# FFN products by one level of Strassen's method, with the activations' sums kept in DRAM

## The chip, the cores and the metric

The kernel runs on one core of a Trainium2 chip. The metric is the device time of one execution in microseconds (us). The engines are named as the profile names them: PE is TensorE, DVE is VectorE, ACT is ScalarE, POOL is GpSimd, SP is SyncE; PEld is PE's weight load, which overlaps its matmuls.

## What is computed

One layer: attention and a state-space mixer in parallel, then the FFN that the change is about, on 1280 tokens (1024 latent, 256 context), D_MODEL 1024 and D_FF 2816.

```python
def ffn_sublayer(x, shift, scale, gate, g_pre, g_post, w_gate, w_up, w_down):
    h = rms_norm(x, g_pre) * (1 + scale) + shift
    f = (jax.nn.silu(h @ w_gate) * (h @ w_up)) @ w_down
    return x + gate * rms_norm(f, g_post)
```

All of it is float32. The kernel gets that precision from float32r operands in two parts: each value is split into a rounded `hi` and a rest `lo`, and a product is three matmuls, hi by hi, lo by hi and hi by lo, summed in PSUM (`split3`, L404 to L408). ACT makes the hi part by a copy, DVE the lo part by a subtraction.

## The kernel before

The phases run one after another, each with one instruction stream an engine, ordered by semaphores. A phase ends when all its engines have ended.

**Output projection** (`phase_out_proj`, L1650). Ten token tiles of 128. For each, PE does 48 matmuls of 512 columns into `psY`. ACT squares and sums (L1743), DVE scales and adds the residual into `y` (L1777, L1781), SP stores `y`, ACT squares again (L1748), and DVE writes the normalised tile to `facc` (L1786). POOL makes the two powers in between (L1719, L1721).

**FFN** (`phase_ffn`, L1805). First the normalised tiles are transposed and modulated: `Turn` has 24 steps (three token blocks of 512, 512 and 256 by eight K tiles); a step is two to four transposes on PE (L148), one ACT (L159) and two DVE instructions (L167, L169). Eight steps stand before the first product, the rest are woven into the first F tiles. Then a loop runs over eleven pairs of F tiles (`over_pairs`). Each F tile of 128 multiplies all tokens: for each block, gate and up, eight K tiles by three matmuls into `psG`; ACT takes the silu (L1886), DVE multiplies (L1920), and both split the result (L1888, L1923). After a pair come 20 down products of six matmuls with 512 columns into `psF`, which DVE adds to `facc` (L1938). SP loads the weights of the pair to come as soon as DVE has taken the lo part of the last.

**Final** (`phase_final`, L1995). The down products of the last pair, ten tiles of 12 matmuls; DVE adds them to `facc` (L2054), ACT squares, POOL makes the power (L2036), DVE scales (L2068), and DVE and POOL in turn add the residual that SP has loaded from `y1` (L2012). SP stores the rows.

## Time and profile before

| | |
|---|---|
| median of 3 runs | 1998.24 us (1996.91 to 2000.24) |
| span of the profiled execution | 1999.9 us |
| PE busy | 1822.0 us (91%), 9587 instructions |
| DVE busy | 900.2 us (45%) |
| ACT busy | 538.4 us (27%) |
| POOL busy | 111.5 us (6%) |
| DMA | 130.97 MB, mean 65 GB/s |
| mean granted TensorE clock | 0.964 |

The span runs from the first to the last instruction of one profiled execution; it lies 1.7 us over the median and within the three runs. Busy times are shares of the span. A matmul's row is longer than the time until the next one begins, since matmuls overlap in the array: the pace of PE is read from the starts, or from something that recurs once a tile. The granted clock is a share of 2.4 GHz; its two levels are 1.00 and 0.50. A releaser (`<-`) is what an engine's idle time ended on.

### The profile page before, as it was taken

The numbers are of one execution on the slowest core, as the hardware profiler recorded it, in microseconds if no ns is written. First come the engines' busy times: TensorE is split into PE (matmuls) and PEld (weight loads), VectorE is DVE, ScalarE is ACT, GpSimd is POOL, SyncE is SP. The second block draws the span as 40 slices with busy tenths as digits, with TensorE's granted clock in tenths as the row PEclk, the third lists the DMA queues.
The fourth block names the chain that finished last, engine by engine and source line by source line (L and its number), as shares of the span: only waits on it lengthen the run. The fifth ranks groups of instructions, "written<-read, shape, count | busy, mean of one in ns | idle before, by whom it ended". The sixth has DMA issues, their size and how long they took to land. (4 is left out here: it accounts for less than half of the span.)

```text
span 1999.9 us, 23563 instructions
## 1 busy us (share of the span) xinstructions
PE 1822.0 (91%) x9587; PEld 1549.0 (77%) x9596; DVE 900.2 (45%) x1240; ACT 538.4 (27%) x770; POOL 111.5 (6%) x130
## 2 busy tenths in 40 slices
PE   5899999778858989986988999999999999999995
PEld 5688888656647777875867888888888888888884
DVE  6635753267754454445445414334143242332418
ACT  5442222132334343443324111111111112011112
POOL 1000000213300000000100000000000000000005
PEclk8899999878979999998999999999999999999997
DMA  8423322110040000005321010010100100001006
GB/s 282 157 86 128 135 95 80 48 47 18 28 147 17 1 12 1 1 1 189 120 102 64 32 64 32 31 56 19 51 31 31 63 31 31 31 31 63 11 25 227
DMA packets 66854, 130.97 MB, mean 65 GB/s; under 512 B 7232, under 2 KB 40592, under 8 KB 66784
## 3 DMA queue, kind: packets, MB, share of 16 engines
q1 hardware_dynamic: 62176, 122.52, 17.8%
q0 software_dynamic: 4608, 7.47, 1.1%
q8 instruction: 50, 0.82, 0.2%
q14 instruction: 20, 0.16, 0.0%
HBM read 108.87 MB, written 21.09 MB: 65 GB/s over the span
## 5 line engine op out<-in xcount | busy, mean ns | idle before, releaser
L406 PE MATMUL psG<-h_hi,gu_hi 128*128 128x512 f32 (+1 forms) x1056 | 373.9, 354 | 0.0
L407 PE MATMUL psG<-h_lo,gu_hi 128*128 128x512 f32 (+1 forms) x1056 | 373.6, 354 | 0.0
L408 PE MATMUL psG<-h_hi,gu_lo 128*128 128x512 f32 (+1 forms) x1056 | 373.5, 354 | 0.0
L406 PEld LDWEIGHTS psG<-h_hi,gu_hi 128*128 128x128 f32 x1056 | 199.7, 189 | 27.9
L407 PEld LDWEIGHTS psG<-h_lo,gu_hi 128*128 128x128 f32 x1056 | 199.7, 189 | 27.8
L408 PEld LDWEIGHTS psG<-h_hi,gu_lo 128*128 128x128 f32 x1056 | 199.6, 189 | 27.5
L1920 DVE TENSOR_TENSOR hid<-hid,psG 128x512 f32<-128x512 f32 (+1 forms) x66 | 39.5, 599 | 359.2 <-ACT hid L1886 359.2
L1938 DVE TENSOR_TENSOR facc<-facc,psF 128x512 f32<-128x512 f32 x180 | 122.9, 687 | 94.3 <-PE psF L408 94.3
L406 PE MATMUL psP<-hT_hi,win_hi 128*128 128x512 f32 (+1 forms) x456 | 163.0, 357 | 0.8 <-DVEq L678 0.8
L407 PE MATMUL psP<-hT_lo,win_hi 128*128 128x512 f32 (+1 forms) x456 | 161.7, 355 | 0.0
L408 PE MATMUL psP<-hT_hi,win_lo 128*128 128x512 f32 (+1 forms) x456 | 161.7, 354 | 0.0
L406 PE MATMUL psF<-d_hi,h_hi 128*128 128x512 f32 x400 | 155.7, 389 | 0.0
L407 PE MATMUL psF<-d_lo,h_hi 128*128 128x512 f32 x400 | 155.7, 389 | 0.0
L408 PE MATMUL psF<-d_hi,h_lo 128*128 128x512 f32 x400 | 155.6, 389 | 0.0
L1886 ACT ACTIVATE hid<-psG 128x512 f32<-128x512 f32 (+1 forms) x66 | 34.8, 527 | 392.3 <-PE psG L408 392.3
L1878 ACT ACTIVATE d_hi<-raw_d 128x1024 fp32r<-128x1024 f32 x22 | 23.3, 1060 | 290.8 <-PE psF L408 241.4
L406 PEld LDWEIGHTS psP<-hT_hi,win_hi 128*128 128x128 f32 x456 | 86.5, 190 | 13.7 <-DVEq L678 1.2
L407 PEld LDWEIGHTS psP<-hT_lo,win_hi 128*128 128x128 f32 x456 | 86.5, 190 | 12.0
L408 PEld LDWEIGHTS psP<-hT_hi,win_lo 128*128 128x128 f32 x456 | 86.3, 189 | 12.2
L1442 DVE TENSOR_TENSOR pt_lo<-psPT,pt_hi 128x512 fp32r<-128x512 f32 (+1 forms) x104 | 57.9, 582 | 78.4 <-ACT pt_hi L1347 78.4
L408 PEld LDWEIGHTS psF<-d_hi,h_lo 128*128 128x128 f32 x400 | 75.1, 188 | 15.6
L406 PEld LDWEIGHTS psF<-d_hi,h_hi 128*128 128x128 f32 x400 | 75.1, 188 | 15.4
(327 smaller groups left out, 3192.0 us busy)
## 6 DMA issues: line engine op xcount, KB each, us to landing
m_wring<-in_w_mod SPq DMA_DIRECT2D x24, 1024.0 KB, 5.8
raw_gu<-in_w_gate SPq DMA_DIRECT2D x22, 512.0 KB, 4.2
raw_gu<-in_w_up SPq DMA_DIRECT2D x22, 512.0 KB, 5.4
raw_d<-in_w_down SPq DMA_DIRECT2D x22, 512.0 KB, 3.9
win_raw<-in_w_in SPq DMA_DIRECT2D x19, 512.0 KB, 6.0
y_scratch<-op_y SPq DMA_DIRECT2D x10, 512.0 KB, 2.9
fi_y<-y_scratch SPq DMA_DIRECT2D x10, 512.0 KB, 5.0
n_xin<-in_x_sample SPq DMA_DIRECT2D x8, 512.0 KB, 9.2
```

The source lines that it names most:

```text
L406: pe.matmul(out, w_hi, x_hi, start=first, stop=False)
L407: pe.matmul(out, w_hi, x_lo, start=False, stop=False)
L408: return pe.matmul(out, w_lo, x_hi, start=False, stop=last)
L1442: dve.tensor_tensor(pt_lo[:, g[0]:g[-1] + 1, r:r + P], psPT[:, (g0 + i) % 2, 0:len(g), :], pt_hi[:, g[0]:g[-1] + 1, r:r + P].bitcast(F32), ...
L1878: act.activation(d_hi[:, s, :], raw_d[:], ACT.Copy).then_inc(d_hi_r, 1)
L1886: act.activation(hid[:, n % 2, :w], psG[:, n % 2, 0, :w], ACT.Silu).then_inc(silu, 1)
L1920: dve.tensor_tensor(hid[:, n % 2, :w], hid[:, n % 2, :w], psG[:, n % 2, 1, :w], ALU.mult).then_inc(h_full, 1)
L1938: dve.tensor_tensor(L.facc[:, t, cols], L.facc[:, t, cols], psF[:, r % 4, :], ALU.add).then_inc(flushed, 1)
```

## The change

**The scheme.** `phase_ffn` and `phase_final` become one phase. Tokens, K and F are halved (`TH` = 640 tokens, four K tiles, `FH` = 11 F tiles) and the eight products of halves become seven by Strassen's method in Winograd's form. The gate and up products become, for each of 22 F tiles, seven products `r` of four K tiles by two token chunks of 320 columns by three matmuls; several of them add to one PSUM bank. F tiles are taken in the order 0, 11, 1, 12, ..., where an odd `n` completes a pair `m`. The down product becomes seven stages `s` of 11 F tiles by five token tiles by three matmuls with 512 columns, summed over all F in PSUM, and so needs no addition for each pair.

**Operands.** `phase_out_proj` transposes and modulates each token tile (`turn`, `modulate`, raw to `L.hraw`), and POOL makes one sum from it (`pair`). At the start of the FFN phase ACT and DVE split the seven token operands `V` (2560 columns each), and POOL and DVE make three further sums. The weight sums of each F tile are DVE's (`sums`), in a single buffer `raw`. Split weights go through a ring of three (`wv`).

**Through DRAM.** When an odd tile is done, POOL makes four sums of the pair's activations (`hs`) and stores seven variants (`L.hv`), 320 KB each. The down stages load them back, with `w_down` in the first four stages; POOL makes the weight sums in the last four.

```diff
 def phase_out_proj(L):
...
+            def pair(u):
+
+                pool.wait_ge(modulated, u + HT + 1)
+                b12, b22 = flat(L.hraw[:, 1, 0, u, :, :]), flat(L.hraw[:, 1, 1, u, :, :])
+                pool.tensor_tensor(b12, b22, b12, ALU.subtract).then_inc(paired, 1)
+                pool.wait_ge(paired, 2 * u + 1)
+                pool.tensor_tensor(b12, b12, flat(L.hraw[:, 0, 0, u, :, :]), ALU.add).then_inc(paired, 1)
...
+            def modulate(t):
+                act.wait_ge(turned, t + 1)
+                g = int(t >= NT_LAT)
+                for k in range(KD):
+                    op = act.activation(L.hraw[:, t // HT, k // 4, t % HT, k % 4, :], psT[:, t % 2, k, :], ACT.Identity,
+                                        bias=L.mod[:, 3 * KD + k, g:g + 1], scale=L.scale2[:, k, g:g + 1])
+                op.then_inc(modulated, 1)
...
+            def turn(t):
+                pe.wait_ge(xn_r, t + 1)
+                if t >= 2:
+                    pe.wait_ge(modulated, t - 1)
+                for k in range(KD):
+                    mm = pe.transpose(psT[:, t % 2, k, :], xn[:, t % 2, k * P:(k + 1) * P], L.ident)
+                mm.then_inc(turned, 1)
...
+                if t >= 1:
+                    turn(t - 1)
+            turn(NT - 1)
...
 def phase_ffn(L):
...
         @block.sync
         def _(sp):
...
+            for n, j in enumerate(ORDER):
+                if n >= 1:
+                    sp.wait_ge(wv_lo, by_order(n - 1, 6) + 1)
                 for i, w in enumerate(("w_gate", "w_up")):
...
+                    sp.dma_start(raw[:, i, :, :].rearrange("p a n -> p (a n)"), L.dram[w][j]).then_inc(w_loaded, 16)
...
         @block.gpsimd
         def _(pool):
...
+            for m in range(FH):
+                n = 2 * m + 1
...
+                pool.wait_ge(hid1, 2 * n + 2)
+                pool.wait_ge(hid2, n + 1)
+                pool.dma_start(L.hv[0, m], g1[0]).then_inc(hs_stored, 16)
+                pool.dma_start(L.hv[1, m], g1[1]).then_inc(hs_stored, 16)
+                pool.dma_start(L.hv[6, m], g2[1]).then_inc(hs_stored, 16)
+                pool.tensor_tensor(hs[0], g2[0], g2[1], ALU.add).then_inc(hs_made, 1)
+                pool.wait_ge(hs_made, 4 * m + 1)
+                pool.tensor_tensor(hs[1], hs[0], g1[0], ALU.subtract).then_inc(hs_made, 1)
+                pool.dma_start(L.hv[3, m], hs[0]).then_inc(hs_stored, 16)
+                pool.tensor_tensor(hs[2], g1[0], g2[0], ALU.subtract).then_inc(hs_made, 1)
+                pool.wait_ge(hs_made, 4 * m + 2)
+                pool.tensor_tensor(hs[3], g1[1], hs[1], ALU.subtract).then_inc(hs_made, 1)
+                pool.dma_start(L.hv[4, m], hs[1]).then_inc(hs_stored, 16)
...
+                pool.dma_start(L.hv[5, m], hs[2]).then_inc(hs_stored, 16)
...
+                pool.dma_start(L.hv[2, m], hs[3]).then_inc(hs_stored, 16)
...
         @block.scalar
         def _(act):
...
+            for n in range(FT):
+                for r in range(NP):
+                    evict(n, r)
+                    if n == 0 and r < 4:
+                        v_high(r + 3)
+                    if by_order(n, r) + R < NQ:
+                        w_high(by_order(n, r) + R)
+                    if r == 0 and n >= 1:
+                        gate2(n - 1)
+                    if r == (4 if n == 0 else 2):
+                        gate1(n)
...
         @block.vector
         def _(dve):
...
+            def w_low(q):
+                n, r = divmod(q, NP)
+                sums(n, r)
+                dve.wait_ge(wv_hi, q + 1)
...
+            def evict(n, r):
+                if n >= 2 and r in (1, 6):
+                    dve.wait_ge(hs_made, 4 * (n // 2))
+                    dve.wait_ge(hs_stored, 16 * 7 * (n // 2))
...
+            for i in range(3):
+                w_low(i)
+                v_low(i)
+            dve.tensor_tensor(t1_raw, whole(hblock(1, 1)), whole(hblock(1, 0)), ALU.subtract).then_inc(t_made, 1)
+            for n in range(FT):
+                for r in range(NP):
+                    if r == 0 and n >= 1:
+                        hidden2(n - 1)
+                    if n == 0 and r < 4:
+                        if r == 3:
+                            evict(0, 1)
+                        v_low(r + 3)
+                    if not (n == 0 and r == 1):
+                        evict(n, r)
+                    if by_order(n, r) + R < NQ:
+                        w_low(by_order(n, r) + R)
+            hidden2(FT - 1)
...
         @block.tensor
         def _(pe):
...
+            for n in range(FT):
+                for r in range(NP):
+                    q = by_order(n, r)
+                    pe.wait_ge(wv_lo, q + 1)
+                    if n == 0:
+                        pe.wait_ge(v_lo, r + 1)
+                    for c in range(2):
...
+                        dst = (psA, psC, psA, psD, psA, psA, psD)[r](c)
+                        for k in range(4):
+                            ks = slice(k * P, (k + 1) * P)
+                            mm = split3(pe, dst, wv[:, q % R, 0, ks], wv[:, q % R, 1, ks], V[:, r, 0, k, chunk(c)],
+                                        V[:, r, 1, k, chunk(c)], r in (0, 1, 3) and k == 0, k == 3, r in (2, 4, 5, 6))
+                        mm.then_inc(prod, 1)
```

**POOL, between the output projection and the end.** In the kernel before:

```order
L1721 TENSOR_TENSOR op_rs<-op_ms,op_nh 128x1
L1654 UNCONDITIONAL_BRANCH
L2029 UNCONDITIONAL_BRANCH
L2031 MEMSET fi_nh 128x1
L2036 TENSOR_TENSOR fi_rs<-fi_ms,fi_nh 128x1 x2
```

and after the change, from the FFN phase's start through the first pair of F tiles (`hid_variants` is `L.hv`):

```order
L2007 TENSOR_TENSOR hraw<-hraw 128x2560
L2010 TENSOR_TENSOR hraw<-hraw 128x2560
L2020 DMA hid_variants<-hraw 128x640
L2021 DMA hid_variants<-hraw 128x640
L2022 DMA hid_variants<-hraw 128x640
L2023 TENSOR_TENSOR hraw<-hraw 128x640
L2025 TENSOR_TENSOR hraw<-hraw 128x640
L2026 DMA hid_variants<-hraw 128x640
L2027 TENSOR_TENSOR hraw<-hraw 128x640
L2029 TENSOR_TENSOR hraw<-hraw 128x640
L2030 DMA hid_variants<-hraw 128x640
```

POOL had nothing to do in the FFN. Now it has eleven such series, one a pair.

**DVE, in the gate and up products.** In the kernel before, from the loop over pairs:

```order
L1920 TENSOR_TENSOR hid<-hid,psG 128x512
L1923 TENSOR_TENSOR h_lo<-hid,h_hi 128x512
L1919 REGISTER_ALU
L1920 TENSOR_TENSOR hid<-hid,psG 128x256
L1923 TENSOR_TENSOR h_lo<-hid,h_hi 128x256
```

and after the change, one F tile (L2247 is `hidden2` of the tile before, L2227 is `evict(n, 1)`, L2211 the lo part of a weight block):

```order
L2247 TENSOR_TENSOR hraw<-hraw 128x640
L2211 TENSOR_TENSOR gu_ring<-const,gu_ring 128x512
L2227 TENSOR_TENSOR hraw<-hraw,psF 128x320 x2
L2211 TENSOR_TENSOR gu_ring<-raw_gu,gu_ring 128x512 x3
L2233 TENSOR_TENSOR hraw<-hraw,psF 128x320 x2
L2192 TENSOR_TENSOR const<-raw_gu 128x512
L2194 TENSOR_TENSOR raw_gu<-raw_gu 128x512
L2211 TENSOR_TENSOR gu_ring<-raw_gu,gu_ring 128x512
```

The splits of the weights stand between the evictions now, and `evict(n, 1)`, with its waits on POOL's sums and stores, stands ahead of the lo parts for `r` = 4, 5 and 6.

## Rows read from the trace of the kernel before

**Rows 1.** Busy time by stretch, FFN loop: window, length, each engine's busy time (instructions), clock.

```profile
1200.00:1250.00 50.00, 50.00 (x232) 41.81 (x231) 20.38 (x27) 5.96 (x7) 0.00 (x0) 1.00 0.09 32
```

**Rows 2.** Timeline of DVE, FFN loop: start, length, instruction; the block of 256 columns.

```profile
1120.73 0.42 DVE L1920 TENSOR_TENSOR hid<-hid,psG 128x256 f32<-128x256 f32 x1 [3.46 <-ACT hid L1886]
...
1175.47 0.42 DVE L1920 TENSOR_TENSOR hid<-hid,psG 128x256 f32<-128x256 f32 x1 [3.46 <-ACT hid L1886]
...
1203.01 0.42 DVE L1920 TENSOR_TENSOR hid<-hid,psG 128x256 f32<-128x256 f32 x1 [3.46 <-ACT hid L1886]
```

**Rows 3.** Timeline, end of the output projection to the first FFN products.

```profile
1036.64 0.39 PE L408 MATMUL psY<-wo_hi,mix_lo 128*128 128x512 f32 x1
...
1043.60 0.76 DVE L1786 TENSOR_SCALAR facc<-op_y,op_rs 128x1024 f32<-128x1024 f32 x1 [0.66 <-POOL op_rs L1721]
...
1044.72 4.67 PE L148 MATMUL psF<-const,facc 128*128 128x128 f32 x28 [7.69 <-PEq L1654]
1045.07 0.43 SPq L1845 DMA_DIRECT2D raw_gu<-in_w_up  x1
...
1061.38 0.48 PE L406 MATMUL psG<-h_hi,gu_hi 128*128 128x512 f32 x1
...
1066.95 1.91 PE L148 MATMUL psF<-const,facc 128*128 128x128 f32 x16
```

**Rows 4.** Busy time by stretch of 2 us, at the end of the output projection.

```profile
1038.00:1040.00 2.00, 0.00 (x0) 0.00 (x0) 1.13 (x2) 0.18 (x2) 0.55 (x1) 1.00 0.00 0
1040.00:1042.00 2.00, 0.00 (x0) 0.00 (x0) 1.54 (x2) 0.39 (x1) 0.00 (x0) 0.69 0.00 0
...
1046.00:1048.00 2.00, 2.00 (x14) 2.00 (x12) 1.31 (x3) 1.50 (x3) 0.00 (x0) 0.60 0.93 358
```

**Rows 5.** Groups of ACT and DVE instructions by line and shape: busy us, mean ns.

```profile
L1886 ACT ACTIVATE hid<-psG 128x256 f32<-128x256 f32 x22 | 8.4, 384 | 81.8 <-PE psG L408 81.8
L1888 ACT ACTIVATE h_hi<-hid 128x512 fp32r<-128x512 f32 x44 | 27.8, 632 | 33.5 <-DVE hid L1920 33.5
L159 ACT ACTIVATE raw_d<-psF,mod,scale 128x256 f32<-128x256 f32 x8 | 4.3, 561 | 2.5 <-PE psF L148 1.3 <-DVE h_lo L169 1.0
L1920 DVE TENSOR_TENSOR hid<-hid,psG 128x256 f32<-128x256 f32 x22 | 9.3, 421 | 74.4 <-ACT hid L1886 74.4
L1923 DVE TENSOR_TENSOR h_lo<-hid,h_hi 128x512 fp32r<-128x512 f32 x44 | 30.5, 693 | 30.8 <-ACT h_hi L1888 30.8
L1908 DVE TENSOR_TENSOR gu_lo<-raw_gu,gu_hi 128x2048 fp32r<-128x2048 f32 x22 | 50.3, 2288 | 19.6 <-ACT gu_hi L1872 19.6
```

**Rows 6.** Groups of POOL instructions, and its DMA issues, by line and shape.

```profile
L2012 POOL TENSOR_TENSOR fi_out<-fi_out,fi_y 128x1024 f32<-128x1024 f32 x5 | 11.8, 2363 | 0.0
L861 POOL TENSOR_TENSOR decayed<-sf,dt_cdrow 128x512 f32<-128x512 f32 x9 | 9.4, 1040 | 14.5 <-DVEq L1053 14.5
L521 POOL DMA_DIRECT2D staged_scratch<-conv_acc x2 | 1.1, 564 | 0.0
```

**Rows 7.** DMA issues: count, KB of each, median us from issue to landing.

```profile
raw_gu<-in_w_up SPq DMA_DIRECT2D x22, 512.0 KB, 5.4
...
kv_scratch<-xbcT POOLq DMA_DIRECT2D x1, 1280.0 KB, 6.1
...
out_ckv<-cache_in POOLq DMA_DIRECT2D x1, 256.0 KB, 2.9
```

**Rows 8.** Timeline of the final phase: POOL and DVE at once.

```profile
1968.18 2.40 POOL L2012 TENSOR_TENSOR fi_out<-fi_out,fi_y 128x1024 f32<-128x1024 f32 x1
...
1968.85 2.81 DVE L1645 TENSOR_TENSOR fi_rows<-fi_rows,fi_b 128x1024 f32<-128x1024 f32 x1
```

**Rows 9.** Timeline: the last gate and up matmul, and DVE's last instructions.

```profile
1942.79 0.28 PE L408 MATMUL psG<-h_hi,gu_lo 128*128 128x256 f32 x1
...
1995.61 1.23 DVE L2012 TENSOR_TENSOR fi_out<-fi_out,fi_y 128x1024 f32<-128x1024 f32 x1
```

More of the change, by code:

```diff
@@ new lines, in phase_ffn, with at @@
+    R = 3
+    ORDER = [j for f in range(FH) for j in (f, f + FH)]
+    NP = 7
+    base = nc.sbuf_base
+    def at(name, offset, shape, dt=F32):
+        return nc.alloc_sbuf_tensor_at(name, shape, dt, offset=offset)
+    V_BYTES = NP * 2 * 4 * TH * 4
+    o_v = (base + 31) // 32 * 32
+    o_raw = o_v + V_BYTES
+    o_ring = o_raw + 2 * D * 4
+    o_u2 = o_ring + R * 2 * 512 * 4
+    assert o_u2 + TH * 4 <= nc.sbuf_top
+    V = at("gv", o_v, [P, NP, 2, 4, TH], F32R)
+    raw = at("raw_gu", o_raw, [P, 2, 2, 512])
@@ new lines, in phase_ffn @@
+    g2 = [lot[:, 2, :], lot2[:, 1, :]]
+    p1_main = lot2[:, 2, :]
+    hs = [lot3[:, i, :] for i in range(4)]
+    o_wd = o_v + 40960
+    hr = at("d_hid", o_v, [P, 3, TH])
+    hh = at("d_hid_ring", o_v + 7680, [P, 3, 2, TH], F32R)
+    wr = at("d_w_ring", o_v + 23040, [P, 3, 2, 512], F32R)
+    wd = [at(f"d_w{i}", o_wd + i * 22528, [P, FH, 512]) for i in range(4)]
+    rows = at("fi_rows", o_wd + 4 * 22528, [P, 2, D])
+    junk = at("fi_sq", o_wd + 4 * 22528 + 8192, [P, 512])
+    yin = at("fi_y", o_raw, [P, 2, D])
@@ new lines, in keep, with squares @@
+            def keep(s):
+                for u in range(HT):
+                    g = HT * s + u
+                    act.wait_ge(dprod, HT * (FH * s + FH - 1) + u + 1)
+                    if s == 0 and u == 0:
+                        act.wait_ge(hs_stored, 16 * 7 * FH)
+                    dst = {0: acc_a, 2: acc_b, 3: acc_c}[s]
+                    act.activation(dst[:, u, :], d_bank(g), ACT.Copy).then_inc(ev_a, 1)
+            def squares(t):
+                u, late = t % HT, t >= HT
+                act.wait_ge(c_done, 2 * t + 2)
+                for col, x in ((ssa, (acc_d, acc_a)[late]), (ssb, (acc_b, acc_c)[late])):
+                    if t >= 1 or col is ssb:
+                        act.wait_ge(sq, 2 * t + (col is ssb))
+                    act.activation(junk[:], x[:, u, :], ACT.Square, accum_out=col[:, t:t + 1]).then_inc(sq, 1)
@@ L2048, in _ @@
+            act.wait_ge(prod, 2 * by_order(FT - 1, 1) + 2)
+            for e in range(3):
+                highs(e)
+            for e in range(NE):
+                s, f = divmod(e, FH)
+                if f == FH - 1 and s in (0, 2, 3):
+                    keep(s)
+                if e + 3 < NE:
+                    highs(e + 3)
+                if s == 5 and 3 <= f < 3 + HT:
+                    squares(f - 3)
+            for t in range(HT, NT):
+                squares(t)
         @block.vector
@@ new lines, in hidden2 @@
+            def hidden2(n):
+                dve.wait_ge(silu2, n + 1)
+                dve.wait_ge(c22, 2 * n + 2)
+                dve.tensor_tensor(g2[n % 2], g2[n % 2], up2, ALU.mult).then_inc(hid2, 1)
+            for i in range(3):
+                w_low(i)
[13 more added lines that the diff above has]
+                        w_low(by_order(n, r) + R)
@@ new lines, in mean, with finish @@
+            def mean(t):
+                dve.wait_ge(sq, 2 * t + 2)
+                dve.tensor_tensor(ms[:, t:t + 1], ssa[:, t:t + 1], ssb[:, t:t + 1], ALU.add).then_inc(row_ready, 1)
+                dve.wait_ge(row_ready, 4 + t + 1)
+                dve.tensor_scalar(ms[:, t:t + 1], ms[:, t:t + 1], 1.0 / D, EPS, ALU.mult, ALU.add).then_inc(ms_r, 1)
+            def finish(t):
+                u, late, g = t % HT, t >= HT, int(t >= NT_LAT)
+                dve.wait_ge(rs_r, t + 1)
+                if t >= 3:
+                    dve.wait_ge(stored[t % 3], 16 * (t // 3))
+                for i, x in enumerate(((acc_d, acc_a)[late], (acc_b, acc_c)[late])):
+                    half = slice(512 * i, 512 * i + 512)
+                    dve.scalar_tensor_tensor(out[:, t % 3, half], x[:, u, :], rs[:, t:t + 1], rows[:, g, half],
+                                             ALU.mult, ALU.mult).then_inc(yt, 1)
+                dve.wait_ge(yt, 2 * t + 2)
+                dve.wait_ge(y_loaded[t % 2], 16 * (t // 2 + 1))
+                dve.tensor_tensor(out[:, t % 3, :], out[:, t % 3, :], yin[:, t % 2, :], ALU.add).then_inc(y_r, 1)
@@ new lines, in _ @@
+            for e in range(3):
+                lows(e)
+            for e in range(NE):
+                s, f = divmod(e, FH)
+                if f == FH - 1 and s in (1, 4, 5):
+                    for u in range(HT):
+                        add(s, u)
+                if e + 3 < NE:
+                    lows(e + 3)
+                if s in (4, 5, 6) and 1 <= f <= HT:
+                    join(s - 1, f - 1)
+                if s == 4 and f == 6:
+                    dve.wait_ge(row_loaded, 64)
+                    for g in range(2):
+                        dve.tensor_tensor(rows[:, g, :], rows[:, g, :], out[:, 0, :], ALU.add).then_inc(row_ready, 1)
+                        dve.wait_ge(row_ready, 2 * g + 1)
+                        dve.tensor_tensor(rows[:, g, :], rows[:, g, :], out[:, 1, :], ALU.mult).then_inc(row_ready, 1)
+                        dve.wait_ge(row_ready, 2 * g + 2)
+                if s == 5 and 4 <= f < 4 + HT:
+                    mean(f - 4)
+                if s == 6 and 2 <= f < 2 + HT:
+                    finish(f - 2)
```

574 lines of the change are left out of this document (330 added, 244 removed).

## The prediction, made before the changed kernel was run

> **What bounds the kernel now.** I read the busy times by stretch first. In the FFN loop PE is busy for all 50.00 us of a window at clock 1.00, DVE for 20.38, ACT for 5.96, POOL for none [rows 1]. So PE's pace is the time there, and what leaves PE is gained, as long as nobody makes it wait. The pace is best read from what recurs on DVE: the block of 256 columns comes 27.54 us after the same block of the F tile before, and 82.28 us after that of the pair before [rows 2]. A pair is two F tiles and the down products, so 120 down matmuls take 82.28 - 55.08 = 27.20 us, 0.2267 us each at 512 columns. An F tile has 96 matmuls of 512 and 48 of 256 columns; the latter take (27.54 - 21.76) / 48 = 0.1204 us. Then I read the two edges. From the last output matmul (start 1036.64, plus one pace: 1036.87) to the first FFN product (1061.38) PE lacks products for 24.5 us [rows 3]. From the last gate and up matmul (1942.91) to the end of the span, 1999.9, are 57.0 us, of which 27.2 are down products: 29.8 us of overhead [rows 9].
>
> **What the change takes from PE.** Gate and up: 22 x 7 x 24 = 3696 matmuls of 320 columns. The shape isn't in the trace; between 0.1204 and 0.2267 us, linear in columns, it is 0.1470 us. That is 3.53 us a product, 24.7 a tile, 543.3 in all. Down: 7 x 11 x 15 = 1155 matmuls at 0.2267 us, 261.8. Together 805.1, before 11 x 82.28 = 905.1: **-100.0 us**. This holds only while ACT and DVE keep up. Durations for the new shapes are drawn through the rows [rows 5]: DVE 0.69 us at 512 columns, 0.83 at 640, 2.82 at 2560, 0.49 for 320 from PSUM; ACT 0.63, 0.74, 2.3 and 0.44. A tile costs DVE eleven of 512 (four sums, seven lo parts), eight of 320, one of 640: 12.3 of 24.7 us. ACT's 8.5 us fit too. As shares nothing is short; the waits decide.
>
> The Trainium skill (TensorE: Matmul & The Clock Gate, Back-to-back issue gap) gives N / 2.4 GHz plus 2.5 ns at full clock, 136 ns for 320 columns and 41 us less in all. By that rule 256 columns would take 109 ns; the trace's 120.4 disagrees, so the sum goes by the rows.
>
> **The wait on even tiles.** `evict(n, 1)` for n = 2, 4, ... 20 waits until POOL has made the four sums of the pair before and all seven stores have landed. DVE stands in that wait, and behind it on DVE are the lo parts of the weights for `r` = 4, 5, 6. PE has only `r` = 1, 2, 3 of the tile in the ring. From the end of product (n, 0), called zero:
> - POOL starts at 3.0: 0.2 lag of the matmul's end, ACT's eviction 0.44, its weight split 0.63 (queued ahead of the silu), silu 0.74, DVE's `hidden2` 0.83, handovers 0.15.
> - The series is serial on POOL. Four sums of 640 columns: a plain sum of 1024 took 2.36 us, one with a broadcast operand 1.04 at 512 [rows 6], so 1.3 to 1.5; I take 1.46, as both operands are full here: 5.8. Six issues ahead of the last store's landing at 0.56 each [rows 6]: 3.4. Handovers 0.2. The last store lands 2.9 us after issue, as 256 KB did; 1280 KB took 6.1 [rows 7], which bounds three stores in flight together at 1.5 us more. Sum 12.3, to 15.3.
> - DVE's two evictions 0.95, the lo part 0.69: PE resumes at 17.0.
> - PE ran dry at 3 x 3.53 = 10.6. Wait: **6.4 us**, between 5.2 and 8.5.
>
> An idle PE also loses its clock. After the last output matmul the granted clock was 1.00 in the first window, 0.69 in the second, half until work had come back for 2.9 us (0.60 in 1046 to 1048, work from 1044.72) [rows 3, 4]. Work at the 1.2 GHz level for 2.9 us is 1.45 us lost. So 7.9 us a tile, ten tiles: **+79 us**, 52 to 100. Odd tiles don't wait: POOL is done by then. Their next hazard is the single weight buffer: the load goes out 1.5 us after product (n-1, 3), lands 5.8 later with both issues [rows 7], two sums and a lo part bring it to 9.4, and PE wants it at 10.6. Covered by 1.2 us.
>
> **The start of the FFN.** Before: 24.5 us plus 48 transposes woven in later at 0.119 [rows 3], 30.2. After: 64 transposes ahead of the last output product, 7.6; the chain to the normalised tile 7.5; the last turn at half clock 1.5; eight modulations of 128 columns, some 0.45 each below the 0.56 for 256 [rows 5], 3.5; POOL's `pair` 2.5; then the weights can be asked for, 6.1 to landing; ACT's weight split and V split, 2.9; DVE's 2.8. Sum 34.8: **+4.6 us**.
>
> Then the first tile: DVE owes two weight sums or one, a lo part and a V part for each product, some 4.2 us against PE's 3.5, and POOL's two sums of 2560 columns (5.8 us each) start in the middle. In the final phase DVE took 2.81 us for an instruction of 1.23 while POOL was in a sum, and ended 1.1 us after it [rows 8, 9]: the two exclude each other. With that DVE reaches the lo parts of product 3 at 28.7 us after the first product's start, of product 6 at 42.6, and the next tile's weights, asked for only then, are split at 50.5. PE's own work until there is 24.7. Waits of 25.9 and a clock loss of 1.4: **+27.3 us**; if POOL and DVE ran side by side, 11.6 less.
>
> The Trainium skill (SBUF — State Buffer, Who interferes with whom) says that a DVE instruction with two SBUF inputs and a GpSimd one that reads SBUF block each other for a whole instruction, and that one SBUF input doesn't. The trace's 2.81 us agrees.
>
> **From gate/up to down.** PE needs `c12`, silu, the hi and lo parts of the first tile, all after the last product: 0.2 + 0.49 + 0.74 + 0.74 + 0.63 + 0.69 and handovers, 4.0 us, and a clock loss of 1.4: **+5.4 us**.
>
> **Down stages.** Each step of 3.4 us asks 1.5 of DVE, 1.4 of ACT, up to 1.2 of POOL and 576 KB. Loads are asked for three steps ahead (10 us) and land in some 5.4: covered. In stage 6 the `finish` of five tiles (2.6 us each), `join` and lo parts ask DVE for 4.9 a step; the ring gives some 4 us, and the first `yin` reload waits behind SP's last load. POOL's shifts for stages 4 to 6 come in one burst that locks DVE. I take **+8 us**, 0 to 15.
>
> **The end.** After the last product five tiles are left on DVE: 0.9 for the additions, then mean and `finish` of 2.9 each, some 1.5 for residual loads, 3.1 for the store and the end: 21.1 against 29.8: **-8.7 us**.
>
> Sum: -100.0 + 4.6 + 79 + 27.3 + 5.4 + 8 - 8.7 = **+15.6 us**. On the profiled execution 2015.5; that lies 1.7 over the median, so 2013.8 on the median, **2014 us**.
>
> **The rivals.**
> 1. Faster: POOL's series is shorter than I make it. What counts is 10.7 us for it, where I have 12.3: from there ten stalls cost under 63 us and the kernel is no slower. The cheaper sum of 1.04 at 512 speaks for it, the full operands against. With 4.4 us a tile, no clock loss, and no exclusion at the start: 2014 - 35 - 12 = 1967. Chance 0.20.
> 2. The series is hidden altogether (the order on DVE leaves PE enough): 2014 - 79 = 1935. The three-deep ring speaks against it: 10.6 us cannot hold 17. Chance 0.06.
> 3. Slower still: the weight load misses its 1.2 us. If it lands 2.6 later than the median, each of 22 tiles waits 1.4: +31, 2045. The stores of POOL may delay it on even tiles only, since they are over by then. Chance 0.16.
> 4. The skill's matmul gap: 41 us less, 1973. The row for 256 columns speaks against it. Chance 0.02.
>
> **How the numbers follow.** The forecast has 0.56, with its own range of 1992 to 2036 from the bounds above. A difference within 0.2% (1994.2 to 2002.2) can't be told from none. The forecast gives faster 0.03, same 0.06, slower 0.47; rival 1 gives 0.17 and 0.03; rivals 2 and 4 0.08 faster; rival 3 0.16 slower. Faster 0.28, same 0.09, slower 0.63. For 8 in 10 the range reaches to rival 1 below and into rival 3 above: 1967 to 2042.
>
> **What would show it.** In the new profile, matmuls of 320 columns start 0.147 us apart; PE idles once every two F tiles, ahead of `r` = 4, for 5 to 8 us, released by DVE's L2211, and DVE's L2227 there by a store or POOL; the clock falls each time. The first tile takes some 50 us. A pair of tiles takes 57 us rather than 49.4. If pairs take 50 us, rival 1 or 2 holds; if odd tiles wait too, on `raw_gu` loads, rival 3.

## The result and the profile after

| | before | after |
|---|---|---|
| median, us | 1999.2 (1996.9 to 2008.8, 4 runs) | 2030.5 (2028.5 to 2035.7, 4 runs) |
| ratio to before | | 1.0156, 95% interval 1.0128 to 1.0184 |
| span of the profiled execution, us | 1999.9 | 2033.9 |
| PE busy, us | 1822.0 | 1752.0 |
| DVE, ACT, POOL busy, us | 900, 538, 112 | 1041, 715, 298 |
| DMA, MB | 130.97 | 182.07 |
| mean granted clock | 0.964 | 0.933 |

The changed kernel is 1.6% slower. The forecast was 2014 us, slower: the direction and the mechanism hold, and 2030 lies in the range, but the loss is twice the one forecast (+31 us against +16).

**Where PE stands still.** Timeline of the changed kernel, one even F tile in the loop: start, length, instruction, idle time ahead of it and its releaser. It answers [rows 2].

```profile
1388.61 0.83 DVE L2247 TENSOR_TENSOR hraw<-hraw 128x640 f32<-128x640 f32 x1 [2.93 <-ACT hraw L2117]
...
1390.00 0.54 POOL L2020 DMA_DIRECT2D hid_variants<-hraw  x1 [47.99 <-DVE hraw L2247]
...
1395.37 1.57 POOL L2027 TENSOR_TENSOR hraw<-hraw 128x640 f32<-128x640 f32 x1
1396.90 1.54 POOL L2029 TENSOR_TENSOR hraw<-hraw 128x640 f32<-128x640 f32 x1
...
1399.47 0.54 POOL L2034 DMA_DIRECT2D hid_variants<-hraw  x1
...
1402.77 0.89 DVE L2227 TENSOR_TENSOR hraw<-hraw,psF 128x320 f32<-128x320 f32 x2 [12.74 <-issue]
1403.58 2.10 DVE L2211 TENSOR_TENSOR gu_ring<-raw_gu,gu_ring 128x512 fp32r<-128x512 f32 x3
```

```profile
1397.14 0.31 PE L409 MATMUL psF<-gv,gu_ring 128*128 128x320 f32 x1
1404.31 0.64 PE L407 MATMUL psF<-gv,gu_ring 128*128 128x320 f32 x1 [6.86 <-DVE gu_ring L2211]
```

DVE stands 12.7 us in L2227, the wait for POOL's sums and stores, from the moment at which POOL starts until 3.3 us after its last store is issued. PE has three products in the ring, and then idles for 6.86 us. The waits of the whole run, grouped (total, times, longest), show it ten times:

```profile
DVE hraw L2227 <- issue: 128.0, 10, 13.0
...
PE psF L407 <- DVE gu_ring L2211: 71.6, 11, 7.2
```

(One of the eleven lies in the first tile.) The clock, in stretches of 2 us, answers [rows 4]; the columns are those of [rows 1]:

```profile
1398.00:1400.00 2.00, 0.00 (x0) 0.00 (x0) 0.00 (x0) 0.00 (x0) 2.00 (x4) 1.00 0.27 105
1400.00:1402.00 2.00, 0.00 (x0) 0.00 (x0) 0.00 (x0) 0.00 (x0) 0.01 (x1) 0.76 0.95 358
1402.00:1404.00 2.00, 0.00 (x0) 0.00 (x0) 1.23 (x3) 0.31 (x1) 0.00 (x0) 0.50 0.08 28
1404.00:1406.00 2.00, 1.69 (x6) 1.69 (x7) 1.55 (x3) 0.95 (x2) 0.00 (x0) 0.50 0.00 0
1406.00:1408.00 2.00, 2.00 (x10) 2.00 (x9) 0.00 (x0) 0.02 (x1) 0.00 (x0) 0.53 0.52 141
1408.00:1410.00 2.00, 2.00 (x16) 2.00 (x15) 0.49 (x1) 0.63 (x2) 0.00 (x0) 1.00 0.87 348
```

PE works at the 1.2 GHz level from 1404.3 to 1407.9. The same resumption recurs every 58.0 us from the fourth on (58.3 to 58.7 before), where 336 matmuls at the pace of 0.1467 us take 49.3: a pair loses 8.7 us, 6.86 idle and 1.87 by the clock.

**The start of the FFN.** POOL's two sums and DVE, timeline, to be held against [rows 8]:

```profile
1073.07 6.07 POOL L2007 TENSOR_TENSOR hraw<-hraw 128x2560 f32<-128x2560 f32 x1 [11.46 <-DVE gv L2183]
1073.62 6.07 DVE L2211 TENSOR_TENSOR gu_ring<-raw_gu,gu_ring 128x512 fp32r<-128x512 f32 x1
...
1082.50 6.04 POOL L2010 TENSOR_TENSOR hraw<-hraw 128x2560 f32<-128x2560 f32 x1 [3.36 <-DVE gv L2183]
...
1083.06 6.03 DVE L2211 TENSOR_TENSOR gu_ring<-raw_gu,gu_ring 128x512 fp32r<-128x512 f32 x1
```

A lo part of 0.69 us lasts as long as POOL's sum: DVE begins it and gets no further until POOL has ended. The first product starts at 1073.13, the second tile at 1122.13, so the first takes 49.0 us:

```profile
1073.13 0.60 PE L407 MATMUL psF<-gv,gu_ring 128*128 128x320 f32 x1 [17.15 <-DVE gv L2183]
...
1122.13 0.61 PE L407 MATMUL psF<-gv,gu_ring 128*128 128x320 f32 x1 [3.64 <-DVE hraw L2237]
```

**The down stages.** Groups by line and shape from 1894 to 1914 (busy us, mean ns), and the timeline near the end:

```profile
L2049 POOL TENSOR_TENSOR d_w<-d_w,d_w 128x512 f32<-128x512 f32 x11 | 19.2, 1783 | 0.0
L2273 DVE TENSOR_TENSOR d_w_ring<-d_w,d_w_ring 128x512 fp32r<-128x512 f32 x5 | 8.8, 1768 | 0.0
L2270 DVE TENSOR_TENSOR d_hid_ring<-d_hid,d_hid_ring 128x640 fp32r<-128x640 f32 x4 | 7.6, 1909 | 0.0
```

```profile
1975.91 13.19 SPq L1982 DMA_DIRECT2D d_hid<-hid_variants  x4
1990.93 0.34 SPq L1997 DMA_DIRECT2D out_sample<-fi_out  x1
1991.32 0.43 SPq L1999 DMA_DIRECT2D fi_y<-y_scratch  x1
...
1989.23 1.41 DVE L2317 SCALAR_TENSOR_TENSOR fi_out<-hraw,cols,fi_rows 128x512 f32<-128x512 f32 x2
1996.53 1.23 DVE L2321 TENSOR_TENSOR fi_out<-fi_out,fi_y 128x1024 f32<-128x1024 f32 x1 [5.89 <-DMA fi_y<-y_scratch]
...
1999.23 0.76 PE L407 MATMUL psF<-d_w_ring,d_hid_ring 128*128 128x512 f32 x1 [5.23 <-DVE d_w_ring L2273]
```

POOL makes 24 weight sums in a row, 1873.7 to 1915.4, and while it does, DVE's parts take 1.77 and 1.91 us where they take 0.68 and 0.82 alone; a sum of POOL takes 1.78 there and 1.29 alone. A step of DVE then has a spacing of 5.2 us where PE needs 3.4, and PE falls dry, for 1.5 and 1.6 us, and once more for 0.9. Near the end DVE waits 5.9 us for a residual tile that SP asks for only behind its last load of the stages and the clearing of old semaphores; behind that wait stand lo parts, and PE idles for 5.2 us, with the clock at 0.50 after it. From the first down matmul (1735.13) to the end of the last (2012.5) are 277.4 us, against 261.8 at pace. Of this, 1.7 us belong to the handover from the gate and up products: PE idles for 3.6 us ahead of 1735.13, and the granted clock is 0.50 from 1735.6 to 1739.0:

```profile
1735.13 0.47 PE L407 MATMUL psF<-d_w_ring,d_hid_ring 128*128 128x512 f32 x1 [3.63 <-DVE d_w_ring L2273]
```

```profile
1737.00:1739.00 2.00, 2.00 (x6) 1.57 (x5) 2.00 (x2) 0.00 (x0) 1.92 (x2) 0.51 1.01 353
```

### The profile page after: what moved, and what is told of

Read it like the earlier page. It is cut to its first block and busy times, and to the rows that moved or that the text cites. A ratio compares the mean times of both kernels' runs of the same rounds, so it can differ in the third digit from the quotient of the medians.

```text
span 2033.9 us, 25129 instructions
## 1 busy us (share of the span) xinstructions
PE 1752.0 (86%) x9950; PEld 1561.8 (77%) x9959; DVE 1041.4 (51%) x1468; ACT 714.6 (35%) x1176; POOL 298.2 (15%) x302
## 2 busy tenths in 40 slices
DMA packets 87317, 182.07 MB, mean 90 GB/s; under 512 B 10048, under 2 KB 43408, under 8 KB 87200
## 5 line engine op out<-in xcount | busy, mean ns | idle before, releaser
L407 PE MATMUL psF<-gv,gu_ring 128*128 128x320 f32 x1232 | 395.4, 321 | 102.4 <-DVE gu_ring L2211 71.6
L408 PE MATMUL psF<-gv,gu_ring 128*128 128x320 f32 x1232 | 392.0, 318 | 0.0
L409 PE MATMUL psF<-gv,gu_ring 128*128 128x320 f32 x1232 | 391.6, 318 | 0.0
L407 PEld LDWEIGHTS psF<-gv,gu_ring 128*128 128x128 f32 x1232 | 242.3, 197 | 106.6 <-DVE gu_ring L2211 74.5
L408 PEld LDWEIGHTS psF<-gv,gu_ring 128*128 128x128 f32 x1232 | 242.5, 197 | 0.0
L409 PEld LDWEIGHTS psF<-gv,gu_ring 128*128 128x128 f32 x1232 | 241.4, 196 | 0.0
L407 PE MATMUL psF<-d_w_ring,d_hid_ring 128*128 128x512 f32 x385 | 152.1, 395 | 13.2 <-DVE d_w_ring L2273 13.2
L408 PE MATMUL psF<-d_w_ring,d_hid_ring 128*128 128x512 f32 x385 | 151.6, 394 | 0.0
L409 PE MATMUL psF<-d_w_ring,d_hid_ring 128*128 128x512 f32 x385 | 151.5, 394 | 0.0
L2088 ACT ACTIVATE gu_ring<-raw_gu 128x512 fp32r<-128x512 f32 x132 | 82.5, 628 | 186.4 <-PE psF L409 138.5
L2211 DVE TENSOR_TENSOR gu_ring<-raw_gu,gu_ring 128x512 fp32r<-128x512 f32 x132 | 101.0, 772 | 68.3 <-ACT gu_ring L2088 64.8
L2270 DVE TENSOR_TENSOR d_hid_ring<-d_hid,d_hid_ring 128x640 fp32r<-128x640 f32 x77 | 81.1, 1054 | 82.6 <-ACT d_hid_ring L2140 82.6
L2140 ACT ACTIVATE d_hid_ring<-d_hid 128x640 fp32r<-128x640 f32 x77 | 57.0, 740 | 150.6 <-PE psF L409 143.1
L407 PEld LDWEIGHTS psF<-d_w_ring,d_hid_ring 128*128 128x128 f32 x385 | 73.4, 191 | 30.8 <-issue 8.5
L2020 POOL DMA_DIRECT2D hid_variants<-hraw x11 | 6.1, 552 | 545.4 <-DVE hraw L2247 545.4
```

Of the source, the lines that this page charges most:

```text
L407: pe.matmul(out, w_hi, x_hi, start=first, stop=False, skip_group_check=onto)
L408: pe.matmul(out, w_hi, x_lo, start=False, stop=False, skip_group_check=onto)
L409: return pe.matmul(out, w_lo, x_hi, start=False, stop=last, skip_group_check=onto)
L2088: act.activation(wv[:, q % R, 0, :], block_of(r, n), ACT.Copy).then_inc(wv_hi, 1)
L2140: act.activation(hh[:, e % 3, 0, :], hr[:, e % 3, :], ACT.Copy).then_inc(h_hi, 1)
L2211: dve.tensor_tensor(wv[:, q % R, 1, :], block_of(r, n), wv[:, q % R, 0, :].bitcast(F32), ALU.subtract).then_inc(wv_lo, 1)
```

## The experiments

All were compared with the kernel before on the same chip; ratios have their 95% interval. Up to the output projection all kernels are alike, but the profiled executions reach its last matmul at anything from 1036.5 to 1049.0 us. So stages are compared by their own lengths, and totals by medians.

### e1: the eviction later in DVE's order

```diff
...
+                    if r == 4 and n >= 2 and n % 2 == 0:
+                        evict(n, 1)
-                    if not (n == 0 and r == 1):
+                    if r != 1 or n % 2:
                         evict(n, r)
```

> Edit: in even F tiles from the third on, DVE takes the eviction of product r = 1 (with its wait on POOL's sums and stores) after the lo part for r = 6 instead of ahead of that for r = 4, and ACT takes its silu at r = 4. Theory (the place of the wait in DVE's order costs 8.7 us a pair: 6.86 of idle PE and 1.87 of clock): PE has products r = 4, 5 and 6 in hand while DVE waits, the idle of 6.9 us vanishes, a pair takes 49.3 to 50.5 us instead of 58.0, and the whole is 75 to 87 us shorter: 1943 to 1955 us, faster than before. Rival (ring, single weight buffer or POOL's traffic limit the pair anyway, and the wait only comes out somewhere else, such as at the next tile's weights): a pair keeps over 54 us and the kernel stays above 1990.

Measured: 2005.6 us, 1.0037 (1.0020 to 1.0055). The rival holds: the gain on the changed kernel, 25 us, is under a third of the one expected, the pair still takes 55 to 57 us, and PE idles for 4.1 to 5.8 us at the next tile's start. One such place, timelines of POOL, SP, DVE and PE:

```profile
1436.88 0.54 POOL L2034 DMA_DIRECT2D hid_variants<-hraw  x1
...
1436.81 0.47 SPq L1971 DMA_DIRECT2D raw_gu<-in_w_up  x1
...
1444.22 0.89 DVE L2229 TENSOR_TENSOR hraw<-hraw,psF 128x320 f32<-128x320 f32 x2 [7.80 <-DMA hid_variants<-hraw]
...
1445.65 0.61 PE L407 MATMUL psF<-gv,gu_ring 128*128 128x320 f32 x1 [4.13 <-DVE hraw L2235]
```

With PE no longer stopped, SP asks for the next 1 MB of weights at the same moment as POOL issues its last three stores. The last store lands 7.3 us after its issue instead of 3.3, and it is this landing that DVE waits for (the second half of the load, issued at 1436.81, lands in the same moment, 1444.19). In the changed kernel PE's stop had kept the two apart.

### e2: one more sum in POOL's series

```diff
-                pool.tensor_tensor(hs[3], g1[1], hs[1], ALU.subtract).then_inc(hs_made, 1)
+                pool.tensor_tensor(hs[3], g1[1], hs[1], ALU.subtract).then_inc(again, 1)
+                pool.wait_ge(again, m + 1)
+                pool.tensor_tensor(hs[3], g1[1], hs[1], ALU.subtract).then_inc(hs_made, 1)
```

> Edit: POOL makes the last of its four sums of a pair twice, one after the other; nothing else changes. Theory (POOL's serial sums and issues end the wait, so each us there is a us of the pair): one more sum of 640 columns is 1.58 us and some 0.1 of handover, PE's idle grows from 6.86 to 8.5 us, ten pairs cost 16 to 18 us: 2046 to 2049. Rival (the landing of the earlier stores ends the wait, or the wait has slack): under 5 us, 2030 to 2035.

Measured: 2049.3 us, 1.0263 (1.0231 to 1.0294), and PE's idle in the loop is 8.5 us each time instead of 6.9:

```profile
1405.05 0.64 PE L407 MATMUL psF<-gv,gu_ring 128*128 128x320 f32 x1 [8.49 <-DVE gu_ring L2214]
```

This is at the upper end of what was expected. The series has no slack: 1.6 us more on POOL are 1.6 us more of PE's idle.

### e3: POOL's start sums left out

```diff
-            pool.wait_ge(v_lo, 1)
-            pool.tensor_tensor(whole(hblock(0, 0)), whole(hblock(1, 0)), whole(hblock(0, 0)), ALU.subtract
...
-                    dve.wait_ge(t34_made, 2)
```

> Leaves out part of the computation: POOL's two sums of 2560 columns at the start of the FFN phase and the waits on them, so that token operands 4 and 5 are split from unsummed values. Theory (POOL and DVE exclude each other there; two DVE lo parts of 0.7 us take 6.07 us): the first F tile takes 37 to 39 us instead of 49.0, the whole 10 to 12 us less: 2018 to 2021. Rival (the first tile is bound by ACT's and DVE's own splits of 2560 columns and POOL's sums lie beside them): 0 to 3 us less.

Measured: 2013.3 us, 1.0072 (1.0044 to 1.0100). The first tile takes 38.0 us instead of 49.0, as expected; 2.8 us more come out of the tiles behind it. The median falls by 17 us, where 10 to 12 were expected; the last 3.5 of them lie in no stage of the FFN's gate and up products.

### e4: PE kept busy in the wait

```diff
+                    if r == 3 and n >= 2 and n % 2 == 0:
+                        for i in range(40):
+                            pe.matmul(ps[:, 6, 0:TC], V[:, 0, 0, 0, 0:P], V[:, 0, 0, 0, 0:TC], start=True, stop=True)
```

> Edit: after product r = 3 of every even F tile from the third on, PE does 40 more matmuls of 320 columns (5.9 us) into a PSUM bank that nobody reads, in the time in which it waits for DVE; nothing else changes. Theory (the idle time costs the clock too, 3.4 us of work at the lower level after each resumption): the granted clock stays at 1.00, the pair goes from 58.0 to 56.2 us, the whole 15 to 19 us less: 2011 to 2015. Rival (the clock falls by its own, or the wait grows by what the clock gives): 0 to 4 us less.

Measured: 2014.0 us, 1.0073 (1.0053 to 1.0093). 400 matmuls of no use make the kernel 16 us faster. PE still waits, for 1.0 to 2.0 us behind them:

```profile
1505.74 0.42 PE L407 MATMUL psF<-gv,gu_ring 128*128 128x320 f32 x1 [1.11 <-DVE gu_ring L2211]
```

```profile
1504.00:1506.00 2.00, 0.89 (x7) 0.63 (x5) 1.80 (x4) 0.88 (x2) 0.00 (x0) 1.00 0.01 4
```

The clock stays at 1.00 through nine of the ten places (behind the longest of these idles, 1.97 us, it fell to 0.50 for 3.4 us), and the last five pairs take 56.5 us. So the idle time cost 1.6 us a pair beside itself, where the account above has 1.87.

### e5: waits on what is read, not on the whole series

```diff
...
-                    dve.wait_ge(hs_made, 4 * (n // 2))
-                    dve.wait_ge(hs_stored, 16 * 7 * (n // 2))
+                    dve.wait_ge(hs_made, 4 * (n // 2) if n % 2 else 4 * (n // 2) - 1)
+                    dve.wait_ge(own_stored, 16 * 3 * (n // 2))
```

> Edit: the three stores that read the gate and up results themselves get a semaphore of their own, and DVE's evictions into them wait for these three and for the sums that read them (three of four on even tiles) instead of for all four sums and all seven stores. Order and work stay. Theory (in the changed kernel the last store's landing, 6 us after the third sum, ends the wait, and in e1, where DVE waited 7.8 us for a store after 3.3 in the changed kernel, it was that landing, delayed by the weight load beside it): DVE resumes 5.8 us earlier, PE's idle goes from 6.87 to about 1 us, the clock stays, a pair takes 50.3 to 51.5 us instead of 58.0, the whole is 63 to 77 us shorter: 1954 to 1968 us. Rival (POOL's sums decide, or the landing of the first stores): a pair over 55 us and above 2000.

Measured: 1958.9 us, 0.9805 (0.9773 to 0.9837), within the range expected and faster than the kernel before. DVE now goes on when POOL ends the third sum, 7.0 us after POOL's first issue instead of 12.8, and PE idles for 1.63 us:

```profile
1362.68 1.59 POOL L2030 TENSOR_TENSOR hraw<-hraw 128x640 f32<-128x640 f32 x1
...
1364.31 0.89 DVE L2231 TENSOR_TENSOR hraw<-hraw,psF 128x320 f32<-128x320 f32 x2 [6.97 <-POOL hraw L2030]
...
1366.38 0.41 PE L407 MATMUL psF<-gv,gu_ring 128*128 128x320 f32 x1 [1.63 <-DVE gu_ring L2215]
```

What made the changed kernel slower than the one before was neither Strassen's products nor the traffic through DRAM as such; it was two semaphores that covered more than they had to.

### e6: the even tile's sum and stores ahead

It contains e5's edit, and after the odd tile it makes the two sums that DVE waits for ahead of the last.

```diff
+                pool.wait_ge(hid1, 2 * n)
+                pool.wait_ge(hid2, n)
+                pool.dma_start(L.hv[0, m], g1[0]).then_inc(own_stored, 16)
+                pool.tensor_tensor(hs[2], g1[0], g2[0], ALU.subtract).then_inc(hs_made, 1)
...
+                pool.dma_start(L.hv[5, m], hs[2]).then_inc(hs_stored, 16)
                 pool.wait_ge(hid1, 2 * n + 2)
```

> Edit: e5's, and POOL stores the even tile's gate result and makes and stores the sum that needs the even tile alone while the odd tile runs; after the odd tile the two sums that DVE waits for come ahead of the others. Theory: DVE's wait ends some 5 us after the odd tile's last product, before PE is through the three products in hand; the pair takes PE's own 49.3 us, up to 50.5 with the weight load's margin; 75 to 87 us shorter than the changed kernel: 1943 to 1955 us. Rival (the stores of POOL now meet the weight load of every tile, and the load misses its margin): idle moves to the tiles' starts, a pair over 53 us, above 1980.

Measured: 1942.0 us, 0.9731 (0.9695 to 0.9768), 1 us under the range expected. Ten pairs of the changed kernel, then of e6, the same matmuls, busy time by stretch:

```profile
1149.00:1731.00 582.00, 512.77 (x3363) 510.14 (x3362) 229.85 (x397) 159.90 (x298) 99.13 (x110) 0.94 0.22 78
```

```profile
1142.00:1637.00 495.00, 493.53 (x3362) 492.74 (x3360) 239.11 (x398) 160.66 (x298) 102.90 (x110) 1.00 0.26 91
```

87 us less for the same work: 69.2 us of idle time fall to 1.5, and the matmuls themselves take 19.2 us less, since the clock is 1.00 throughout. This is the price of the wait on even tiles.

### e7: the start sums on DVE

```diff
-            pool.tensor_tensor(whole(hblock(0, 0)), whole(hblock(1, 0)), whole(hblock(0, 0)), ALU.subtract
...
+            dve.wait_ge(v_lo, 3)
+            dve.tensor_tensor(whole(hblock(0, 0)), whole(hblock(1, 0)), whole(hblock(0, 0)), ALU.subtract
+                              ).then_inc(t34_made, 1)
```

(and the second sum likewise)

> Edit: the two sums of 2560 columns at the start of the FFN phase are made by DVE, after its third of such sums, and not by POOL. Theory (POOL and DVE exclude each other: two lo parts of 0.68 us took 6.07 and 6.03 us, so POOL's sums cost DVE 10.7 us; on DVE they cost 2 x 2.81): the first F tile takes 43 to 45 us instead of 49.0, the whole 4 to 6 us less: 2024 to 2027. Rival (no exclusion; e3 gained because less is summed): the first tile takes 49 us or more, up to 5.6 us longer.

Measured: 2020.7 us, 1.0118 (1.0084 to 1.0153); the first tile 41.3 us instead of 49.0, more than the 4 to 6 us expected. DVE, busier than POOL by far, takes over 5.6 us of work, and the kernel gets faster.

```profile
1069.80 0.61 PE L407 MATMUL psF<-gv,gu_ring 128*128 128x320 f32 x1 [16.90 <-DVE gv L2177]
...
1111.11 0.42 PE L407 MATMUL psF<-gv,gu_ring 128*128 128x320 f32 x1 [3.68 <-DVE hraw L2231]
```

### e8: the order behind the last F tile

```diff
+                if e == NE - 2:
+                    put(0)
...
-                if s == 6 and 2 <= f < 2 + HT:
-                    finish(f - 2)
+                if s == 6 and f in (2, 4, 6, 8, 9):
+                    finish((2, 4, 6, 8, 9).index(f))
...
+                if s >= 5:
+                    pool.wait_ge(w_lo, e - 5)
...
+                    if n == FT - 1 and r == 6:
+                        lows(0)
...
-            pe.wait_ge(c12, 2 * FT)
...
+                    if e == 0 and u == 4:
+                        pe.wait_ge(c12, 2 * FT)
```

> Three edits behind the last F tile. (1) SP stores the first output tile and asks for the third residual tile ahead of the last two loads of the down stages, and the five finishes stand two steps apart; theory: PE's idle of 5.2 us near the end goes, 5 to 6.5 us less. (2) POOL's weight sums of the last two stages keep at most five steps ahead of the products instead of coming in one burst; theory: the three idles of 1.5, 1.5 and 0.9 us with their clock loss go, 3 to 5 us less. (3) The hi and lo parts of the first down product are made ahead of the last silu and the last eviction, and PE waits for the last eviction only ahead of the fifth token tile; theory: the idle of 3.6 us between gate/up and down falls under 1, 3 to 5 us less. Sum: 11 to 16 us less than the changed kernel, 2014 to 2019. Rival for (1) and (2) (DVE itself has too much to do in the last stage): the idle near the end stays at 3 us or more.

Measured: 2012.6 us, 1.0071 (1.0041 to 1.0101). All idle times behind the gate and up products are gone. The last gate and up matmul and the first down matmul of e8:

```profile
1729.07 0.31 PE L409 MATMUL psF<-gv,gu_ring 128*128 128x320 f32 x1
1729.21 0.39 PE L407 MATMUL psF<-d_w_ring,d_hid_ring 128*128 128x512 f32 x1
```

The handover costs nothing instead of 3.6 us, and the down stages take 262.8 us instead of 277.4, 1.0 over pace. Of these 14.6 us, 1.7 are the clock behind the handover. So edit 3 gave 5.3 us, where 3 to 5 were expected, and edits 1 and 2 together 12.9, where 8 to 11.5 were; they weren't run apart. The whole, 2012.6, is 1 us under the range expected.

### e10: e1 and e5 together

> The edits of e1 and e5 together: DVE's eviction of product r = 1 comes later on even tiles, and waits only for the sums and stores that read its target. Theory (in e1 the idle of 4.1 to 5.8 us was the last store's landing, delayed by the weight load asked for at the same time; the sums and first stores were long done): the idle at the tiles' starts goes, a pair takes 49.3 to 50.5 us, 1943 to 1955 us. Rival (what e1 lost lies in the order itself: the late eviction delays the splits of the next tile's weights): idle of 3 us or more a pair stays, above 1970.

Measured, in a single execution: 1977.1 us. Gate and up from the second tile on take 551.0 us, against 609.4 in the changed kernel and 543.2 in e5. Neither theory holds alone: nine of the ten idles are shorter than the rival's 3 us, and the time lies above its 1970. Idles of 1.9 us stay (2.7 to 3.8 four times), and now it is the weights that are late:

```profile
1430.75 0.46 SPq L1972 DMA_DIRECT2D raw_gu<-in_w_up  x1
...
1438.21 0.69 DVE L2198 TENSOR_TENSOR const<-raw_gu 128x512 f32<-128x512 f32 x1 [5.22 <-DMA raw_gu<-in_w_up]
```

7.4 us from issue to landing, beside three stores, where the median of the changed kernel is 4.7. So of e1's 4.1 us some 2.2 were the last store's landing and 1.9 the weights; this split is inferred from the two idles. This is rival 3 of the prediction: it doesn't appear in the changed kernel, where PE's stop keeps load and stores apart, and comes out once the stop is gone. In e6 the stores go out earlier, and it is gone.

### e11, e9 and e12: the start once more, and all edits together

e11 is the start alone: the splits of the first two token operands ahead of the weights (which the other edits of the start share), and DVE's start sums one at a time.

```diff
+            for i in range(2):
+                v_low(i)
             for i in range(3):
                 w_low(i)
-                v_low(i)
+            v_low(2)
...
+                    if n == 0 and r == 0:
+                        dve.wait_ge(v_lo, 3)
+                        dve.tensor_tensor(whole(hblock(0, 0)), whole(hblock(1, 0)), whole(hblock(0, 0)), ALU.subtract
```

> The changed kernel with e7's edit, the two sums placed one at a time between the parts of the third to fifth products, and the first two token operands split by ACT and DVE ahead of the first weights, which are still loading then. Theory (DVE's own work bounds the first tile once POOL is out, and it is idle for 5 us ahead of the weights): the first FFN product comes 2 us later or earlier, the second tile 11 to 14 us earlier than in the changed kernel (from the last output product), 4 to 6 of them beyond e7; 2013 to 2018 us. Rival (the load of the second tile's weights, or ACT's parts, bound it): no more than e7's 2021.

Measured: 2022.9 us, 1.0108 (1.0082 to 1.0134), no better than e7. From the end of the last output matmul to the start of the second tile are 76.5 us in the changed kernel, 68.6 in e7 and 73.5 in e11. The rival holds, by ACT's parts: DVE makes a sum, ACT needs 2.3 us for its hi part, and DVE waits for that with nothing else in its order, four times (that this is all of e11's loss against e7 is not shown):

```profile
1095.44 2.83 DVE L2179 TENSOR_TENSOR gv<-hraw,gv 128x2560 fp32r<-128x2560 f32 x1 [2.41 <-ACT gv L2072]
```

> The edits of e6, e7 and e8 together, and three small ones: DVE makes the two start sums one at a time between the products' parts, ACT and DVE split the first two token operands ahead of the first weights, and SP asks for each tile's w_up one product ahead of w_gate. Theory (the waits are separate, so their costs add): the changed kernel's 2030 less 88 (e6), 18 (e8), 8 to 10 (e7) and 4 to 6 for the splits made while the weights load: 1904 to 1916 us, 4% under the kernel before. Rival (the gains overlap, since a wait removed uncovers the next): above 1925.

Measured: 1920.4 us, 0.9598 (0.9571 to 0.9625), 4 us above the expected range. It contains e11's order of the start, with the same four waits (72.1 us to the second tile).

e12 mends that: each sum is made one product earlier than in e9, beside ACT's work on the one before. So is the first eviction of product `r` = 1, and the parts of the second down product are made ahead of the last silu; what each of the three gave wasn't run apart.

```diff
+            dve.wait_ge(v_lo, 3)
+            dve.tensor_tensor(whole(hblock(0, 0)), whole(hblock(1, 0)), whole(hblock(0, 0)), ALU.subtract
+                              ).then_inc(t34_made, 1)
             for n in range(FT):
...
-                        if r == 3:
+                        if r == 2:
                             evict(0, 1)
...
+            lows(1)
             hidden2(FT - 1)
```

> e9 with another order at the FFN's start and one at its end: DVE makes each start sum one product earlier, so that ACT's hi part of the one runs beside DVE's work on another (in e9 DVE waited four times 2.4 us for ACT there), takes the first eviction of product r = 1 one product earlier, and the parts of the second down product are made ahead of the last silu too. Theory (the first tile is bound by the hand to and fro of ACT and DVE, 9.6 us of waits): the second tile starts 6 to 10 us earlier after the last output product than e9's 72.2 us, the idles of 1.6 and 1.1 us behind the gate and up products go, 7 to 12 us less than e9: 1908 to 1913. Rival (DVE's work alone bounds the first tile): under 3 us less, above 1917.

Measured: **1912.1 us, 0.9567 (0.9537 to 0.9597)**, 4.3% under the kernel before. The second tile starts 62.1 us after the last output matmul, 10 earlier than in e9. DVE's waits for ACT between the products' parts are gone but for one of 0.7 us; a wait of 2.8 us for the second tile's weights is left ahead of that tile:

```profile
1070.68 2.82 DVE L2274 TENSOR_TENSOR first_use<-hraw 128x2560 f32<-128x2560 f32 x1
1073.41 2.82 DVE L2276 TENSOR_TENSOR hraw<-hraw 128x2560 f32<-128x2560 f32 x1
1076.15 2.82 DVE L2194 TENSOR_TENSOR gv<-first_use,gv 128x2560 fp32r<-128x2560 f32 x1
```

By medians e12 gains 8 us on e9, by the ratios to the kernel before 6, less than the 10 of that stage.

## Why the prediction was right in kind and short in size

| term, us | forecast | measured |
|---|---|---|
| PE's pace | -100.0 | -101.0 |
| start of the FFN | +4.6 | +6.2 |
| first tile, and what follows of it | +27.3 | +28.8 |
| wait on even tiles | +79 | +87.3 |
| gate/up to down | +5.4 | +5.5 |
| down stages | +8 | +13.7 |
| the end | -8.7 | -8.3 |
| ahead of the changed code | 0 | +1.8 |
| sum | +15.6 | +34.0 |

The profiled spans differ by 34.0, 18.4 more than the forecast. The steps that failed are sizes: the wait on even tiles, +79, measured +87.3, and the down stages, +8, measured +13.7. Each wait was named with its cause; but costs of +116 us and a gain of -100 nearly cancel, and so 14 us too few in these two terms leave half of the loss unforecast.

**The start of the FFN** holds an error of the accounts. The prediction counts 48 transposes woven in behind the first product of the kernel before. The trace has 32; 16 more end at that product (1061.38), so that twelve of the 24 steps stand ahead of it and not eight, and lie within the 24.5 us already counted:

```profile
1058.18 3.44 PE L148 MATMUL psF<-const,facc 128*128 128x128 f32 x16 [7.73 <-DVE gu_lo L1908]
```

So the old start is 28.3 us and not 30.2. The new one measures 34.5 (27.7 to the first product and 6.8 for the transposes in the output projection). The prediction has 34.8, though its items add up to 34.4. Its items for the end, as they are given, add up to 20.0 where it has 21.1; it measures 21.5. Nor does its own range of 1992 to 2036 follow from its bounds: 52 to 100 us for the even tiles alone spans 1987 to 2035.

**PE's pace** held: 320 columns, drawn linearly between the two widths of [rows 2], came out at 0.1467 us for 0.1470. The gap in the Trainium skill's page TensorE: Matmul & The Clock Gate (section Back-to-back issue gap), which the page gives for an isolated matmul, comes to an estimate of 0.136 us; this trace disagrees again. So rival 4 is out.

**The even tiles** are 8.3 of the 18.4 us missed, the sum of ten small errors of one kind. The prediction put POOL's start 3.0 us after product (n, 0) and the series at 12.3; it measures 3.3 and 12.8 (sums of 1.58 instead of 1.46 us, a last landing of 3.3 instead of 2.9). PE's idle is 6.87 instead of 6.4, and the clock's return took 3.6 us of work and not 2.9 as in [rows 4], 1.87 us a pair instead of 1.45. e2, e5 and e6 show the mechanism from three sides, e4 the clock's part. Rivals 1 and 2 are out: with 12.8 us the series lay well beyond the 10.7 from which the kernel would have been no slower.

**The down stages** are the other large miss, 5.7 us. Both of their costs were named, and priced by feeling: "POOL's shifts for stages 4 to 6 come in one burst that locks DVE" and "the first `yin` reload waits behind SP's last load", 8 us together. Worked out, it would have been two stages' sums of POOL without a pause, each holding one part of DVE to its own length, three parts a step, so 5.2 us a step for PE's 3.4 (the length of such a sum, 1.78 us, is the changed kernel's); and for SP the loads up to the last, the clearing and a landing of 5 us, one after another, against a finish that is due before them, with lo parts queued behind it. e8 removes 12.9 of the 13.7.

**The first tile** was right with the exclusion of DVE and POOL worked in: 49.0 us for 50.5. The prediction drew it from one pair of rows [rows 8]; e3 (-11.0 on the tile) and e7 (-7.7, though DVE then does more) show POOL's sums as a cause; how much of e7's gain is the exclusion, and how much that a sum takes DVE 2.82 us and POOL 6.07, was not run apart. The Trainium skill's page SBUF — State Buffer (section Who interferes with whom) says that a DVE instruction with two SBUF inputs and a GpSimd one that reads SBUF exclude each other for a whole instruction. The trace agrees, 6.07 us for an instruction of 0.69.

**Rival 3**, the weight load with 1.2 us of cover, was wrong for this kernel and right as a mechanism: in the loop of the changed kernel DVE's waits for these weights are at most 2.33 us, and PE isn't idle at the start of any tile from the third on. (Ahead of the second, DVE waits 4.23 us for them and PE idles for 3.64; that is part of the first tile's 49.0.) e1 and e10 show where it lay hidden.

What stays open: e10 is one execution, and its split of e1's 4.1 us is that of a single place; the 2 to 4 us that e12 lacks against its stage weren't followed; and the spread of up to 12 us in when the output projection ends, in all kernels, wasn't looked into.
